# RWKV-7 chunk stage: the triangular-inverse levels of both head halves step by step in turn, with the next chunk's preparation moved beside them

## The reference, cut to what matters

```
def _wkv_step(S, inp):
    r, w, k, v, a, b = inp
    sa = einsum('bhvk,bhk->bhv', S, a)
    S = S * w[:, :, None, :] + sa[..., None] * b[:, :, None, :] + v[..., None] * k[:, :, None, :]
    return S, einsum('bhvk,bhk->bhv', S, r)
...
a = sigmoid(aw0 + (xa @ aw1) @ aw2); g = sigmoid(xg @ gw1) @ gw2
decay = exp(-exp(log_w))      # a' = -kk, b' = kk * a, kk = k * k_k divided by its norm
y = groupnorm(y) * ln_w + ln_b + sum(r * k * r_k) * v;  out = (y * g) @ w_o
```

## Time and profile before

| | us |
|---|---|
| median of 3 runs (3676.47 to 3685.97) | 3681.79 |
| the profiled execution | 3688.88 |
| its span | 3687.0 |
| TensorE busy in the span | 3482.2 (94%) |
| VectorE busy | 1735.3 (47%) |
| ScalarE busy | 976.1 (26%) |
| GpSimd busy | 583.1 (16%) |
| chunk stage, first low inverses to last | 591.3 |

### The profile page before, as it was taken

How to read it: one execution, slowest core, us unless ns; L and a number is a source line. 1 busy time by engine, 2 the same in 40 slices (tenths; PEclk the granted TensorE clock), 3 DMA queues, 4 the chain that set the end, 5 groups by cost and what they waited for, 6 DMA issues and landing times.

```text
span 3687.0 us, 62862 instructions
## 1 busy us (share of the span) xinstructions
PE 3482.2 (94%) x24636; PEld 3068.2 (83%) x24636; DVE 1735.3 (47%) x3218; ACT 976.1 (26%) x1832; POOL 583.1 (16%) x243
## 2 busy tenths in 40 slices
PE   9999998999999999998999788888899999999998
PEld 6667666756999999996899777777785799999998
DVE  3544454114544444446203367667631644444445
ACT  2223332511111111112214355556520211111111
POOL 0000000000222222211223122223230122222111
PEclk9999999999999999999999889889969999999999
DMA  3221121610111111102222101000151111111101
GB/s 101 55 74 57 44 71 36 206 58 34 46 46 46 46 46 46 46 1 83 94 71 102 65 13 43 29 25 24 31 176 30 58 46 46 46 46 46 46 29 48
DMA packets 151723, 207.26 MB, mean 56 GB/s; under 512 B 42670, under 2 KB 126689, under 8 KB 151170
## 3 DMA queue, kind: packets, MB, share of 16 engines
q1 hardware_dynamic: 145506, 185.08, 15.3%
q0 software_dynamic: 6048, 19.73, 1.7%
HBM read 174.39 MB, written 50.82 MB: 61 GB/s over the span
## 4 chain that ended last, share of the span: by engine, by line
PE 66%; PEld 6%; DVE 5%; issue 3%; ACT 1%; DMA 1%; SPq 0%; DVEq 0%; ACTq 0%; PEldq 0%; POOL 0%
PE bank L471 64%; PEld bank L471 6%; PE bank L479 2%; DVE hT L2808 1%; DVE arena L2742 1%; DVE arena L2643 1%; SPq L1400 0%; DMA arena<-in_rwkv_a_w 0%; ACT arena L2186 0%; DVE n_lo L2610 0%; DVE arena L2759 0%; DMA arena<-arena 0%; ACT arena L1843 0%; DVE arena L2790 0%; DVE arena L2774 0%
## 5 line engine op out<-in xcount | busy, mean ns | idle before, releaser
L471 PE MATMUL bank<-arena 128*32 128x128 f32 (+15 forms) x8142 | 1172.0, 340 | 89.7 <-DVE hT L2808 27.9
L471 PEld LDWEIGHTS bank<-arena 128*128 128x128 f32 (+7 forms) x8142 | 834.1, 179 | 405.7 <-issue 122.3
L2441 DVE TENSOR_TENSOR hT<-hT,bank 128x384 f32<-128x384 f32 (+1 forms) x816 | 425.7, 526 | 502.1 <-PE bank L471 501.7
L471 PE MATMUL bank<-u_hi,dn_hi 128*128 128x384 f32 (+1 forms) x1536 | 496.0, 326 | 12.6 <-DVE hT L2441 8.3
L471 PE MATMUL bank<-u_lo,dn_hi 128*128 128x384 f32 (+1 forms) x1536 | 497.2, 328 | 0.0
L471 PE MATMUL bank<-n_hi,up_hi 128*128 128x384 f32 (+1 forms) x1536 | 489.6, 325 | 2.2 <-ACT arena L2027 2.2
L471 PE MATMUL bank<-n_lo,up_hi 128*128 128x384 f32 (+1 forms) x1536 | 489.5, 325 | 0.0
L1843 ACT COPY arena<-bank 128x512 f32<-128x512 f32 (+15 forms) x573 | 261.1, 491 | 856.0 <-PE bank L471 603.6
L1675 POOL TENSOR_TENSOR up_lo<-arena,up_hi 128x2048 fp32r<-128x2048 f32 x32 | 147.9, 4622 | 1558.7 <-ACT up_hi L2011 1558.7
L471 PE MATMUL bank<-u_hi,dn_lo 128*128 128x384 f32 (+1 forms) x1536 | 376.2, 326 | 0.0
L2643 DVE TENSOR_TENSOR arena<-arena 128x384 f32<-128x384 f32 (+1 forms) x192 | 163.9, 854 | 435.4 <-ACT arena L2027 435.4
(11 more groups left out here) (208 smaller groups left out, 3950.2 us busy)
## 6 DMA issues: line engine op xcount, KB each, us to landing
arena<-in_ffn_w_up SPq DMA_DIRECT2D x32, 1024.0 KB, 5.5
arena<-in_ffn_w_down SPq DMA_DIRECT2D x32, 1024.0 KB, 7.6
arena<-past_scratch SPq DMA_DIRECT2D x32, 640.0 KB, 8.1
past_scratch<-in_cache_kv_latent SPq DMA_DIRECT2D x128, 128.0 KB, 2.4
hidden_scratch<-hT SPq DMA_DIRECT2D x1, 4288.0 KB, 13.0
past_scratch<-in_cache_k_rope SPq DMA_DIRECT2D x128, 32.0 KB, 2.1
arena<-in_rwkv_w_r SPq DMA_DIRECT2D x4, 1024.0 KB, 8.7
r_scratch<-arena POOLq DMA_DIRECT2D x8, 512.0 KB, 5.6
```

Source lines behind the costliest of these rows:

```text
L471: return pe.matmul(out, lhsT, rhs, start=first, stop=last, skip_group_check=group)
L2441: lane.do(dve.tensor_tensor(hT[:, k, at:at + w], hT[:, k, at:at + w], b[:, 0:w], ALU.add), ring.drained)
```

## The change

On TensorE each level is split into single-step functions. `level_16_first` and `level_16_second`, `level_32_first` and `_second`, `level_64_turned`, `_first` and `_second` of half 0 and half 1 stand in turn, all ahead of finals(0). The results of the two halves need places of their own: X4 becomes two tiles, XT gets a second one (XT_b); X5, W5 and XD32 stay single. `rates(c+1)` stands in the first steps, `key_sums(c+1)` between level steps, `key_scales` in finals(0) ahead of the state product; before_keys(c+1) behind first_sums(1); gates in finals(1), turn_z behind it. Five of nine keep_busy calls go. finals(0) now comes behind turn_bonus, whose bank ScalarE takes behind norms and squares. ScalarE makes both spread_16 of the next chunk at the end of a chunk. GpSimd does `sums_before(c+1)` ahead of `group_norm(c-1)`. VectorE does both halves' level 16 and blocks_32 first; sums ahead of centre; and the first level step of a chunk is the first thing TensorE does in it.

```diff
         zbuf = q(8, P)
-        X4, X5, W5 = q(512), q(1024), q(1024)
+        values_at = q.at
+        X4a, X5, W5, XT_b = q(512), q(512), q(512), q(1024)
...
-        W4 = hx[:, 7168:8192]
+        W4, X4 = hx[:, 7168:7680], [X4a, hx[:, 7680:8192]]
+        XTs = [XT, XT_b]
...
+                level_16_first(c, 0, ma)
                 r_b.wait(pe, c)
                 b_with_r(0, ar)
+                if prepare:
+                    rates(c + 1, wn, 0)
+                    rates(c + 1, wn, 1)
+                level_16_second(0)
+                level_16_first(c, 1, ma)
                 bk_b.wait(pe, c)
                 k_with_both(0, 0, ar)
                 k_with_both(0, 1, ar)
-                level_16(c, 0, ma, lambda: turn_b_k(c, P))
-                level_32(c, 0, ma, lambda: bonus_sums(c, P))
-                bonus_at = ra.filled.n - 1
+                level_16_second(1)
+                keep_busy(ra)
+                level_32_first(c, 0, ma)
+                turn_b_k(c, P, (Bt,))
+                level_32_second(c, 0)
+                bonus_sums(c, P)
+                bonus_at = ra.filled.n
+                level_32_first(c, 1, ma)
+                turn_b_k(c, P, (Kt,))
+                level_64_turned(0)
+                level_32_second(c, 1)
+                if prepare:
+                    key_sums(c + 1, wn)
+                level_64_first(0, ma)
+                level_64_turned(1)
+                level_64_second(0)
+                level_64_first(1, ma)
                 v_in[par].wait(pe, nth)
-                level_64(0, ma, [when(prepare, lambda: key_sums(c + 1, wn)), lambda: first_sums(0), lambda: turn_bonus(P, bonus_at)])
-                finals(0, when(prepare, lambda: rates(c + 1, wn, 0)), when(prepare, lambda: (rates(c + 1, wn, 1), key_scales(c + 1, wn))))
+                first_sums(0)
+                level_64_second(1)
+                turn_bonus(P, bonus_at)
+                finals(0, when(prepare, lambda: key_scales(c + 1, wn)), nothing)
 
                 b_with_r(1, ar)
                 k_with_both(1, 0, ar)
                 k_with_both(1, 1, ar)
-                level_16(c, 1, ma, nothing)
+                keep_busy(ra)
+                rv.wait_drained()
+                first_sums(1)
                 if wn == TAIL:
                     before_keys_tail(AR[1 - par])
                 elif prepare:
                     before_keys(c + 1, AR[1 - par])
-                level_32(c, 1, ma, when(finish, lambda: gates(c - 1, P)))
-                level_64(1, ma, [nothing, lambda: first_sums(1), nothing])
-                finals(1, when(finish, lambda: turn_z(c - 1, P, Y[1 - par])), nothing)
+                finals(1, when(finish, lambda: gates(c - 1, P)), nothing)
+                if finish:
+                    turn_z(c - 1, P, Y[1 - par])
...
+                if prepare:
+                    sums_before(c + 1, wn)
                 if finish:
                     group_norm(c - 1, P, Y[1 - par], vt[1 - par])
-                if prepare:
-                    sums_before(c + 1, wn)
...
# ScalarE, chunk
                     lora_columns(c + 1, wn)
-                tokens(P)
+                    both_rates(c + 1, wn)
                 spread_32(c, 0)
+                spread_turned(0)
                 take_w_32()
+                tokens(P, (Btok,))
+                spread_32(c, 1)
+                take_x_32(0)
                 bonus_out(P)
+                spread_turned(1)
+                take_w_32()
                 if prepare:
                     square_keys(c + 1, wn)
-                take_x_32()
-                bonus_factors(par, P)
-                if finish:
-                    squares(c - 1, P, Y[1 - par])
+                tokens(P, (Ktok,))
                 take_turned()
+                take_x_32(1)
                 take_w_64()
+                take_turned()
+                take_x_64(0)
+                take_w_64()
+                take(P1, P, 512)
+                take_x_64(1)
                 if prepare:
                     norms(c + 1, wn)
                 if finish:
+                    squares(c - 1, P, Y[1 - par])
+                bonus_factors(par, P)
+                take(SA, P, 512)
+                if finish:
                     deviations(c - 1, P)
-                take(P1, P, 512)
-                take_x_64()
-                take(SA, P, 512)
-                if prepare:
-                    both_rates(c + 1, wn)
-                spread_16(c, 1)
                 if prepare:
                     decays(c + 1, wn, wn == TAIL)
+                if prepare:
+                    decays_before(c + 1, wn)
                 take(Y[par][:, 0:512], P, 512)
                 if prepare:
-                    decays_before(c + 1, wn)
                     key_factors(c + 1, wn)
-
-                spread_32(c, 1)
-                take_w_32()
+                take(P1, P, 512)
+                take(SA, P, 512)
                 if wn == TAIL:
                     diagonals_tail()
                 elif prepare:
                     diagonals(c + 1, MA[1 - par])
-                take_x_32()
-                take_turned()
-                take_w_64()
-                take(P1, P, 512)
-                take_x_64()
-                take(SA, P, 512)
+                take(Y[par][:, 512:1024], P, 512)
+                signal(act.drain(), y_b)
                 if finish:
                     z_to_store(c - 1)
-                take(Y[par][:, 512:1024], P, 512)
-                signal(act.drain(), y_b)
                 if wn == TAIL:
                     spread_tail()
                 elif prepare:
                     spread_16(c + 1, 0)
+                    spread_16(c + 1, 1)
...
# VectorE, blocks_32
             def blocks_32(c, d):
+                if d == 1:
+                    xt_b.wait(dve, c, 1)
                 b = ring.bank()
...
# VectorE, chunk
+                if finish:
+
+                    y_b.wait(dve, c - 1)
+                level_16(0)
                 b_with_r()
+                blocks_32(c, 0)
+                level_16(1)
                 k_with_both(0)
                 k_with_both(1)
-                if finish:
-
-                    y_b.wait(dve, c - 1)
-                level_16(0)
+                blocks_32(c, 1)
                 scale_state()
-                blocks_32(c, 0)
+                if prepare:
+                    clamp(c + 1, wn)
+                    sums(c + 1, wn, wn == TAIL)
                 if finish:
                     centre(c - 1, P, Y[1 - par])
                 if prepare:
-                    clamp(c + 1, wn)
+                    inverse_norms(c + 1, wn)
                 if finish:
                     variances(c - 1, P)
                 if prepare:
-                    inverse_norms(c + 1, wn)
+                    normed_keys(c + 1, wn)
+                new_half(0)
                 if finish:
                     scale_outputs(c - 1, P, Y[1 - par])
-                new_half(0)
+
                 if prepare:
-                    normed_keys(c + 1, wn)
-                    sums(c + 1, wn, wn == TAIL)
-
+                    a_keys(c + 1, 1 - par, wn)
                 b_with_r()
+                if prepare:
+                    b_keys(c + 1, wn)
                 k_with_both(0)
                 k_with_both(1)
-                if prepare:
-                    a_keys(c + 1, 1 - par, wn)
-                level_16(1)
-                if prepare:
-                    b_keys(c + 1, wn)
-                blocks_32(c, 1)
```

The step functions do what the levels did before; the first of them:

```diff
+            def level_16_first(c, d, ma):
+                apart(x4_b.sem, c * x4_b.per + d + 1)
+                b = narrow(rv, rv.filled.n - 3)
+                for j in range(8):
+                    for rows, cols in diagonal(8 * d + j):
+                        ins = mm(b[rows, j * 64:(j + 1) * 64], ma[rows, cols], X4[d][rows, j * 64:(j + 1) * 64], True, True)
+                rv.done(ins)
+                drained_at["w4", d] = rv.filled.n
```

More of the change, by code:

```diff
@@ L380, in program @@
         keys_4 = [arena[:, xe_at:xe_at + D], Y[1]]
-        values_4 = [X5, W5]
+        values_4 = [arena[:, values_at:values_at + D], XT_b]
         wo2_01 = Carve(c.at)(2, D)
@@ L1104, in level_16, with level_32_first @@
                 rv.done(ins)
-            def level_32(c, d, ma, filler):
+            def level_32_first(c, d, ma):
                 apart(x5_b.sem, c * x5_b.per + d + 1)
@@ L1113, in level_32, with level_32_second, level_64_turned, level_64_first @@
                 ra.done(ins)
-                w5_at = ra.filled.n
-                filler()
+                drained_at["w5", d] = ra.filled.n
+            def level_32_second(c, d):
                 xt_b.wait(pe, c, d + 1)
-                keep_busy(ra)
-                b = narrow(ra, w5_at)
+                b = narrow(ra, drained_at["w5", d])
                 for j in range(8):
                     for rows, cols in diagonal(j):
```

(55 more changed lines are left out.)

33 lines of the change are left out of this document (14 added, 19 removed).

## The result

The changed kernel takes **3825.0 us** (median of four, 3818.0 to 3827.2) against 3682.7 for the kernel before in the same job: ratio **1.038, interval [1.0364, 1.0396]**, slower by 142 us. I had forecast 3729 (+47) and a range to 3764: the sign was right, the size three times too small.

A forecast was written before the change was run, and what follows sets the result against it. A ring of waits through several engines, none full, was taken to bound the kernel. Period 77.6 + 0.7 (contention) + 3.6 (clock) = 81.9 us, +6.2; with first and last pieces and tail +47, so 3729 us, range 3694 to 3764.

The forecast's parts named there:

- The ring: Chunk stage: a loop of waits through several engines, none full, sets the period, 77.6 us at full clock after the change.
- waits of part 1: TensorE's six named waits, mostly for ScalarE, from the first level step through finals(0): 6.6 us in sum.
- part 1: TensorE from a chunk's first level step to the end of the first half's state product: 32.4 us work, 39.0 with waits.
- part 2: From the first half's state product's end, through VectorE and the low inverses, to the next chunk's first level step: 38.6 us.
- TensorE's gap: TensorE, through at 29.0 us, stands still some 9.6 us in each chunk before the next first level step.
- The shared path: VectorE's a_keys and b_keys beside GpSimd's group norm: +0.7 us a period, bounds -0.8 and +2.3.
- The clock: TensorE at half clock behind its gaps: 3.6 us a period, bounds 0 and 7.2.
- B: Milder rival: clock loss and contention hide in the waits behind them; period 77.6 us, 3697 us in all; chance 0.20.
- C: Faster rival: ScalarE keeps up with the level steps and TensorE stays warm; period 71.0 us, 3645 in all; chance 0.10.
- E: Rival of no change: interleaving only moves waits; period 75.7 us, 3678 in all; chance 0.07.
- D: Harsher rival: contention at its bound and clock loss doubled; period 87.1 us, 3771 in all; chance 0.08.
- No cost for the moved decay sums: GpSimd's decay sums ahead of the group norm: decays_before ends 2.5 us after the state product, before a_keys needs it.

The follow-up runs named there:

- no_norm_fillers: Changed kernel with the group norm's three GpSimd operations on 8 of 1024 columns and more keep_busy matmuls in TensorE's three large gaps: 3763.6 us, 1.0197.
- keys_bonus_fillers: Changed kernel with before_keys and gates ahead of first_sums(1), diagonals ahead of copies, bonus factors ahead of norms, and keep_busy matmuls in three gaps: 3742.8 us, 1.0158.
- products_first: Changed kernel with b_with_r and k_with_both of half 0 ahead of the chunk's first level step again, as in the kernel before: 3835.5 us, 1.0398.

## Why the prediction was wrong in size

The ring was right, and its terms can be set beside the period of 88.9 us shown above:

| step | predicted | measured |
|---|---|---|
| waits of part 1 | 6.6 | 5.7 (1.29, 0.50, 0.93, 0.20, 2.80) |
| part 1 | 39.0, clock apart | 41.9 |
| first_sums(1) starts, in part 2 | 12.2 | 16.1 |
| before_keys' last mask ends | 18.6 | 26.5 |
| low inverses start | 22.9 | 31.2 |
| next level step | 38.6 | 47.0 |
| TensorE's gap | 9.6 | 10.0 |

- **Part 1** held in the shown period. What it has over 39.0 is clock: the solution product, the key scales and the state product took 8.3 us, with 5.0 in no_norm_fillers at full clock.
- **The shared path was sized wrong.** I took +0.7 with a bound of 2.3, one blocked operation. Three operations stand beside three of GpSimd's, and each was blocked: first_sums(1) starts 3.9 us late. The row of a_keys and the rule I set beside it pointed there; I priced one collision and should have priced the row of them.
- **The clock was sized wrong.** I took 3.6, at most 7.2. In the shown period it costs 3.3 in part 1, 1.4 at the first steps, and 4.0 between first_sums(1) and the last mask (10.4 us instead of 6.4): 8.7. The mistake was to scale the old loss: each of the three gaps is followed by a cold stretch of its own, on work that the ring waits for. The Trainium skill, TensorE: Matmul & The Clock Gate, section "HAM oscillation — how this bites in real kernels", warned of gaps that come back every round; the windows above agree, and I had given that rival too little.
- **A term is missing from the sum.** I looked for cold stretches only behind gaps. The fourth one, in part 1, follows no long gap; it lies in half of the pieces and made part 1 of the third 5.7 us longer. What sets it off stays open.
- **Clock and blocking together.** Taken out together they gave 61 to 67 us, one by one 20 to 23 and 23 to 29. That a longer wait lengthens the next gap, so that the two feed one another, would explain it, but is argued and not shown.
- **The pieces.** On the two profiled executions the change costs 135 us, 88 more than I said. The last piece was 95.9 us, not 74: 22 of them. Its part 1 ran at half clock (granted 0.50 from 2741 to 2768). The first piece was 89.0, not 76.8: 12. The six whole ones were 9.1 each over 81.9: 55. The end was 2 less early than I said, and the part ahead of the stage 2 shorter.
- **Rivals.** B (milder), C (faster) and E fell: every named wait was there, and what the clock and the blocking cost did not hide behind it. D had the right mechanism, contention and clock together, and was still too low (87.1 against 91.0 a period); I had given it 0.08. Both of its bounds came from single collisions in a kernel in which they were rare.
- **No cost for the moved decay sums** was wrong in what it left out: alone, that move costs the kernel before 12 to 15 us.

What stays open: no_norm_fillers is still 77 us slower than the kernel before, where the ring at full clock gives +15 (rival B). Its pieces account for the 62: the six whole ones take 84.9 us instead of 77.6 (44), the first 84.4 instead of 73.8 (11), the last 78.1 instead of 71.1 (7). Seven of them have the cold stretch in part 1. At the 5.7 us that it cost in the changed kernel that would be some 40 us, an estimate; what the added matmuls themselves cost is not told apart from it. Why the clock falls in that busy stretch, in some pieces and not in others with the same waits, is open.

## What to carry over

Before two halves are interleaved, ask what the second half's work was hiding: here it hid 13.7 us of inverses on VectorE, and taking it forward put them on the ring. Price every gap that a new order makes with the clock that follows it, and every run of two-operand VectorE work with all the GpSimd operations beside it, not with one. When pieces of one loop differ in length, compare a long one with a short one before the mean is explained. And look for cheap cover in the old kernel first: nine more keep_busy matmuls a chunk, in two waits, gave 0.3%, where the large change lost 3.8%.

## What the runs showed of the hardware

- A chain of GpSimd operations beside a chain of VectorE ones delays both: VectorE's 1.24 us became 2.0 to 3.4, GpSimd's 2.35 became 3.2. Masks, with a bank as one input, stayed at 0.62 to 0.65 each beside it.
- More clock is not less time: 0.82 to 0.90 gave nothing where the fillers ran 3 us past the moment at which the next step's input was ready (keys_bonus_fillers), 0.90 to 0.96 gave 12 us in the kernel before.
- The clock can fall without a long gap: granted 0.64 over 19 us in which TensorE was 98% busy, behind 23 us of small matmuls with waits of 0.2 to 1.3 us (no_norm_fillers), and 0.50 over 17 us in the changed kernel itself. With the same steps and waits it falls in some pieces and not in others.
- The same operation of the low inverses (L2926, 128x512) took 1.1 us in the shown period of the changed kernel, 3.55 in another (at 2706.70), and 4.4 in a run beside GpSimd work (products_first): this kind of blocking lengthens the inverses too, which no step of mine had priced.
